# The wait between an up and a down projection: down units begin on ten of eleven hidden tiles

## The chip, the core and the metric

The kernel runs on one core of a Trainium2 chip. Such a core has TensorE (PE in the profile) for matmuls, VectorE (DVE), ScalarE (ACT), GpSimd (POOL) and SyncE (SP), each with its own stream of instructions; they meet at semaphores, and DMA queues bring data from the chip's main memory. The metric is the time of one execution in microseconds on the device; less is better.

## The reference

Two layers of a diffusion backbone over 512 latent tokens and 256 context tokens, of width 1024. Each layer mixes tokens in four parallel branches and then runs a feed-forward network. Only that last part matters here:

```python
def swiglu(u, w_gate_up, w_down):
    gate, up = jnp.split(u @ w_gate_up, 2, axis=-1)
    return (jax.nn.silu(gate) * up) @ w_down

for l in range(DEPTH):                      # DEPTH = 2
    with_ctx = l < DEPTH - 1
    ...
    u = modulate(rmsnorm(h, g_ffn_pre[l]), mod[3], mod[4])
    h = h + mod[5] * rmsnorm(swiglu(u, w_gate_up[l], w_down[l]), g_ffn_post[l])
    if with_ctx:
        ...
        hc = hc + modc[5] * rmsnorm(swiglu(uc, w_gate_up[l], w_down[l]), g_ffn_post[l])
```

The hidden width is 2816, which is 22 tiles of 128. Layer 0 works on all 768 tokens, layer 1 on the 512 latent ones.

## The kernel before

**Numbers in two halves.** Every large product is made of three matmuls: activations and weights are each split into a high part (a copy to the 4-byte type that PE reads fast) and a low part (the value minus the high part), and PE adds high x high, low x high and high x low. This is `chunk_product` (L787 is its matmul), for one block of 128 input rows `k` and one output tile.

**Weight units.** Weights come in units of up to 128 x 2048 values. SP's DMAs bring a unit into one of two raw buffers; ACT makes `w_hi` (L1278) and DVE makes `w_lo` (L1725). Both are in a helper `split(g, it, s)` that each engine has, and that always prepares the unit after the one named: the split of unit u + 1 stands at the head of unit u's work and waits until the products of unit u - 1, which used the same buffer, are done (`acc_ready`) and the transfer has landed. SP brings the unit after that when DVE's `w_lo` has freed the raw buffer.

**The feed-forward stages.** The hidden width is worked in two halves of 11 tiles, so a layer has the phases up0, down0, up1, down1. An up unit (11 in a phase) makes the gate tile (j = 0) and the up tile (j = 1) of one hidden tile. ACT takes SiLU of the gate out of PSUM (L1310), DVE multiplies it with the up tile (L1752), POOL then copies the product to `hid_hi` (L2414), subtracts to get `hid_lo` (L2416) and counts up `hid_split`. A down unit (8 in a phase) makes one output tile of 128 channels from the 11 hidden tiles of its half, in 11 row blocks. Its result is copied out by ACT in down0 (L1342) and added by DVE in down1 (L1779).

**What sets the order.** There is no scheduler: each engine's program is written out, phase by phase. At the end of a phase ACT, DVE and POOL meet at a barrier (`Phases.end`: each counts up `others_end` and waits for all three and for PE). PE only drains and goes on when another product phase follows (`end_products`). Before a down phase PE waits for `hid_split` to reach `g.h0`, the number of all hidden tiles made so far, so for the last tile of the up phase as well (L916). Inside a phase, `pairs` runs units in a hardware loop of two units a turn; with `peel` the first two units are straight code ahead of the loop. PE's products use two accumulators in turn, which ACT or DVE set free (`acc_free`).

**Background.** The up0 phase of layer 0 also computes part of the next layer's modulation: DVE sums, and PE's small matmuls (L770) close each unit and the phase.

Places that the change and the prediction touch: `gemm_unit` and `gemm` of PE, ACT and DVE, `split` of ACT and DVE, and the barrier.

Of the kernel before, what the change touches and what calls it, by code (L numbers as in the profile page):

```python
# [233 lines left out]
def build(nc, x, c, ctx_in, c_ctx, w_mod, b_mod, g_mix_pre, g_mix_post, g_ffn_pre, g_ffn_post, w_in, a_sink,  # L234
# [4 lines left out]
    with stack:  # L239
# [507 lines left out]
        def _(pe):  # L747
# [57 lines left out]
            def gemm_unit(g, it, s, bk, at):  # L805
# [4 lines left out]
                for j in range(g.nt):  # L810
# [3 lines left out]
                    if not early:  # L814
                        if g.t0 >= 2 or t >= 2:
                            pe.wait_ge(acc_free[t % 2], t // 2 + g.nt * it)
                        for k in range(g.kc):
                            if g.name == "uq_nope" and j == 0:
                                made = g.t0 - HEADS + k
                                pe.wait_ge(acc_free[made % 2], made // 2 + 1)  # L820
                            chunk_product(g, slot, t, j, k)
                            order = gate_order(g.layer)
                            if g.name == "gates1_rest" and j == 0 and 0 <= k - (KD - len(order)):
                                gate_block(order[k - (KD - len(order))])
# [86 lines left out]
            def gemm(groups, bk):  # L911
                if groups[0].name == "w_out":
                    early_unit(groups[0])
                for g in groups:
                    if g.name.startswith("down"):
                        pe.wait_ge(hid_split, g.h0)  # L916
                    if g.name == "branch1":
                        pe.wait_ge(y_split, HEADS * (n.ysp + 1))
                        n.ysp += 1
                    pairs(pe, g, lambda it, s: gemm_unit(g, it, s, bk, g.u0 - groups[0].u0), peel=bk is not None)  # L920
                if bk is not None:
                    for i in bk.rest(sum(g.n for g in groups) - 1):
                        back_unit(bk, 0, i)
# [342 lines left out]
        def _(act):  # L1266
# [12 lines left out]

            def gemm_unit(g, it, s):  # L1280
                l = g.layer
                if not (g.early and isinstance(it, int) and 2 * it + s == 0) or g.name == "w_out":
                    split(g, it, s)
                if g.name == "gates1_rest":
                    act.wait_ge(tr_copied, n.tr)
# [92 lines left out]
                if made == 13:  # L1378
                    act.wait_ge(dup_in, 16 * n.dup)

            def gemm(l, groups):
                if groups[-1].name == "branch1":
                    tok = toks(groups[0].lat)
                    for slot in range(2):
# [16 lines left out]
                for g in groups:  # L1401
                    if g.name == "uq_nope":
                        act.wait_ge(c_spread, l + 1)
                        A(tile_at(C_RSTD, False), ps[:, 6:8, 0:TOK // 2], ACT.Copy).then_inc(c_rstd, 1)
                    pairs(act, g, lambda it, s: gemm_unit(g, it, s), peel=g.kind == "swiglu")
                g = groups[-1]
                if g.kind == "merge" and g.dst[0] != 3:

# [236 lines left out]
            n.lstm_w = 0  # L1645
            for index, (kind, l, arg) in enumerate(phases):
                if kind == "gemm":
                    gemm(l, arg)
                elif kind == "setup":
                    load_vectors(act, 0)  # L1650

# [63 lines left out]
        def _(dve):  # L1715
# [3 lines left out]
            def split(g, it, s):  # L1719

                slot, u = (g.u0 + s + 1) % 2, g.u0 + s + 2 * it + 1
                if isinstance(u, int) and u >= n_units:
                    return
                dve.wait_ge(w_hi_done, u + 1)
                V.tensor_tensor(w_lo[slot][:, :], w_raw[slot][:, :], w_hi[slot][:, :].bitcast(F32),  # L1725
                                ALU.subtract).then_inc(w_lo_done, 1)

            def gemm_unit(g, it, s, bk, at):
                if not (g.early and isinstance(it, int) and 2 * it + s == 0) or g.name == "w_out":
                    split(g, it, s)  # L1730
                if bk is not None:
                    static = isinstance(it, int)
# [549 lines left out]
            for index, (kind, l, arg) in enumerate(phases):  # L2282
# [6 lines left out]
                if kind == "gemm":  # L2289
                    bk = background.get(index)  # L2290
                    for g in arg:
# [8 lines left out]
                            if isinstance(it, int) and g.name != "ukv":  # L2300
                                ropes(arg, g.u0 - arg[0].u0 + 2 * it + s)

                        pairs(dve, g, unit, peel=bk is not None)
                    for i in bk.rest(sum(g.n for g in arg)) if bk is not None else ():
                        back_sums(bk, 0, i)
                elif kind == "setup":
# [220 lines left out]
```

## Time and profile before

| | |
|---|---|
| Median of 3 runs | 3462.56 us (3456.1 to 3471.19) |
| Profiled execution, its own time | 3466.68 us |
| Its span, first to last instruction | 3464.9 us |
| PE busy | 3249.9 us, 94% |
| DVE, ACT, POOL busy | 1690.6, 1082.4, 337.9 us |
| Mean granted clock of PE | 0.958 |

The timeline prints runs of equal instructions as one row: start, duration, engine, line, operation, out <- in with the tile's shape, the count, and in brackets how long the engine stood idle just before and who released it. A granted clock of 1 is 2.4 GHz, 0.5 is 1.2 GHz. "768" or "512" in a shape is the number of tokens: layer 0 or layer 1.

### The profile page before, as it was taken

To read this page: it belongs to the slowest core of one execution; us is meant where nothing else is said; L and a number is where in the kernel's file an instruction comes from. 1 tells how busy PE (TensorE), PEld (TensorE's weight loads), DVE (VectorE), ACT (ScalarE), POOL (GpSimd) and SP (SyncE) were. 2 spreads that over 40 slices of the span, in tenths; PEclk is the share of its full clock that TensorE was granted. 3 is DMA by queue.
4 is the path that set the end of the run, shared out by engine and by line. 5 is a ranking of instruction groups with operands and counts; after the bars stand their busy time and mean duration, and the time that the engine had idled before them with its cause. 6 is when DMAs were issued, how large, how long until landed. Compare 5 with 4: busy or idle time off the path is not lost. (4 is left out here: it accounts for less than half of the span.)

```text
span 3464.9 us, 46710 instructions
## 1 busy us (share of the span) xinstructions
PE 3249.9 (94%) x18308; PEld 2934.4 (85%) x18308; DVE 1690.6 (49%) x3070; ACT 1082.4 (31%) x1806; POOL 337.9 (10%) x252
## 2 busy tenths in 40 slices
PE   7999999999999989899999989999999998889997
PEld 4999988998898789899999988877887886677876
DVE  6645355433376765763121365545433577443334
ACT  3233344333314433211211232334443234322222
POOL 0001100100120010121031000010100210101010
PEclk8999999999999998899999989999999999979998
DMA  5511410320250022432221333141321521332322
GB/s 199 174 40 49 131 50 13 122 61 25 74 189 25 25 95 88 146 121 64 76 61 45 95 128 100 61 122 37 110 61 37 183 67 37 134 97 79 110 80 97
DMA packets 332309, 303.79 MB, mean 88 GB/s; under 512 B 39822, under 2 KB 309852, under 8 KB 330204
## 3 DMA queue, kind: packets, MB, share of 16 engines
q1 hardware_dynamic: 317134, 230.03, 21.3%
q10 hardware_dynamic: 14990, 71.23, 5.4%
q8 instruction: 124, 2.03, 0.2%
q14 instruction: 61, 0.50, 0.0%
HBM read 266.47 MB, written 34.34 MB: 87 GB/s over the span
## 5 line engine op out<-in xcount | busy, mean ns | idle before, releaser
L787 PE MATMUL ps<-u_hi,w_hi 128*128 128x384 f32 (+1 forms) x2352 | 687.3, 354 | 40.9 <-issue 19.3
L787 PE MATMUL ps<-u_lo,w_hi 128*128 128x384 f32 (+1 forms) x2352 | 679.2, 350 | 0.0
L787 PE MATMUL ps<-u_hi,w_lo 128*128 128x384 f32 (+1 forms) x2352 | 678.6, 350 | 0.0
L1725 DVE TENSOR_TENSOR w_lo<-w_raw,w_hi 128x2048 fp32r<-128x2048 f32 x145 | 353.2, 2436 | 431.1 <-ACT w_hi L1278 428.9
L787 PEld LDWEIGHTS ps<-u_hi,w_hi 128*128 128x128 f32 x2352 | 430.2, 190 | 70.8 <-issue 45.0
L787 PEld LDWEIGHTS ps<-u_lo,w_hi 128*128 128x128 f32 x2352 | 434.0, 190 | 22.1
L787 PEld LDWEIGHTS ps<-u_hi,w_lo 128*128 128x128 f32 x2352 | 433.3, 190 | 22.8
L1278 ACT ACTIVATE w_hi<-w_raw 128x2048 fp32r<-128x2048 f32 x145 | 277.5, 1914 | 519.6 <-PE ps L787 293.4
L980 PE MATMUL ps<-u_hi,w_hi 128*128 128x384 f32 (+1 forms) x816 | 311.6, 382 | 4.5 <-ACT space L1485 3.5
L980 PE MATMUL ps<-u_hi,w_lo 128*128 128x384 f32 (+1 forms) x816 | 297.1, 364 | 0.0
L980 PE MATMUL ps<-u_lo,w_hi 128*128 128x384 f32 (+1 forms) x816 | 294.9, 361 | 0.0
L1887 DVE SCALAR_TENSOR_TENSOR space<-space,silu_c 128x256 f32<-128x256 f32 x560 | 247.6, 484 | 9.9
L1342 ACT ACTIVATE space<-ps 128x768 f32<-128x768 f32 (+3 forms) x102 | 76.5, 752 | 469.4 <-PE ps L787 457.7
L1057 PEld LDWEIGHTS ps<-space 128*128 128x128 f32 x1472 | 184.4, 196 | 35.0 <-issue 16.5
L1057 PE MATMUL ps<-space 128*128 128x128 f32 (+1 forms) x1472 | 202.1, 284 | 5.4 <-DVE space L2107 4.9
L2065 DVE TENSOR_REDUCE mx<-ps 128x1 f32<-128x768 f32 (+3 forms) x200 | 156.2, 781 | 101.4 <-PE ps L1015 75.7
L1752 DVE TENSOR_TENSOR space<-space,ps 128x768 f32<-128x768 f32 (+1 forms) x44 | 36.1, 821 | 308.7 <-PE ps L787 301.8
L980 PEld LDWEIGHTS ps<-u_hi,w_hi 128*128 128x128 f32 x816 | 156.5, 192 | 19.5 <-issue 7.3
L787 PE MATMUL ps<-hid_hi,w_hi 128*128 128x384 f32 (+1 forms) x528 | 160.7, 358 | 12.1 <-POOL hid_lo L2416 12.1
L980 PEld LDWEIGHTS ps<-u_hi,w_lo 128*128 128x128 f32 x816 | 155.8, 191 | 11.4
L980 PEld LDWEIGHTS ps<-u_lo,w_hi 128*128 128x128 f32 x816 | 156.6, 192 | 7.5
L787 PE MATMUL ps<-hid_lo,w_hi 128*128 128x384 f32 (+1 forms) x528 | 159.7, 356 | 0.0
(264 smaller groups left out, 4537.2 us busy)
## 6 DMA issues: line engine op xcount, KB each, us to landing
w_raw<-in_w_in SPq DMA_DIRECT2D x288, 256.0 KB, 3.9
space<-in_w_mod SPq DMA_DIRECT2D x48, 1024.0 KB, 5.1
w_raw<-in_w_gate_up SPq DMA_DIRECT2D x176, 256.0 KB, 3.8
w_raw<-in_w_down SPq DMA_DIRECT2D x96, 192.0 KB, 2.7
w_raw<-in_w_branch SPq DMA_DIRECT2D x64, 256.0 KB, 3.4
h_scratch<-space ACTq DMA_DIRECT2D x4, 3072.0 KB, 8.6
space<-h_scratch ACTq DMA_DIRECT2D x4, 3072.0 KB, 10.3
m_scratch<-space ACTq DMA_DIRECT2D x3, 3072.0 KB, 9.8
```

Of the source, the lines that this page charges most:

```text
L787: last = nc.tensor.matmul(ps[:, 2 * (t % 2) + b, 0:a1 - a0], wv[w][:, k, j * P:(j + 1) * P], xx[:, k, a0:a1], start=(k == 0 and w == 0 and ...
L980: last = nc.tensor.matmul(ps[:, fill_bank, 0:cols.stop - cols.start], wv[w][:, k, j * P:(j + 1) * P], xx[:, k, cols], start=k == 0 and m = ...
L1057: last = nc.tensor.matmul(ps[:, 6, h * dv:(h + 1) * dv], pt_buf[i % 2][:, bi * P:(bi + 1) * P], v, start=bi == 0, stop=bi == len(keys) - 1)
L1278: A(w_hi[slot][:, :], w_raw[slot][:, :], ACT.Copy).then_inc(w_hi_done, 1)
L1342: A(tile_at(dst_tile(g, it, s, j), g.lat), acc(t % 2, g.lat), ACT.Copy if g.kind == "copy" else ACT.Sigmoid, scale=HD ** -0.5 if g.name == ...
L1725: V.tensor_tensor(w_lo[slot][:, :], w_raw[slot][:, :], w_hi[slot][:, :].bitcast(F32), ALU.subtract).then_inc(w_lo_done, 1)
L1752: V.tensor_tensor(tile_at(30 + s, g.lat), tile_at(30 + s, g.lat), acc(t % 2, g.lat), ALU.mult).then_inc(hid_ready, 1)
L1887: ins = V.scalar_tensor_tensor(part[:, sg], w, silu_c[:, k, sg:sg + 1], part[:, sg], ALU.mult, ALU.add)
L2065: own.did(V.reduce_max(mx[:, c4:c4 + 1], view, AX))
```

## The change

Three engines change at the four passages from an up phase to a down phase.

- PE: the wait ahead of a down phase is for one tile fewer (`g.h0 - 1`). In the first unit of the phase, ahead of the eleventh row block (`k == HALF - 1`, HALF is 11), PE waits for the last tile (`g.h0`).
- ACT and DVE: the split that stood at the head of the first down unit (it prepares the second down unit) is issued at the end of the up phase, ahead of the barrier: `split_next(after)` in ACT, `split(after, 0, 0)` in DVE. The first down unit leaves its own call out.
- PE, ACT and DVE run the first two units of down0 as straight code ahead of the loop (`peel`), so that the first unit can differ. down1 had no loop before either. down1 of layer 1 and of layer 0 are otherwise treated alike.

```diff
@@ -815,6 +815,8 @@
                         if g.t0 >= 2 or t >= 2:
                             pe.wait_ge(acc_free[t % 2], t // 2 + g.nt * it)
                         for k in range(g.kc):
+                            if g.name.startswith("down") and k == HALF - 1 and isinstance(it, int) and it == s == 0:
+                                pe.wait_ge(hid_split, g.h0)
                             if g.name == "uq_nope" and j == 0:
                                 made = g.t0 - HEADS + k
                                 pe.wait_ge(acc_free[made % 2], made // 2 + 1)
@@ -913,11 +915,12 @@
                     early_unit(groups[0])
                 for g in groups:
                     if g.name.startswith("down"):
-                        pe.wait_ge(hid_split, g.h0)
+                        pe.wait_ge(hid_split, g.h0 - 1)
                     if g.name == "branch1":
                         pe.wait_ge(y_split, HEADS * (n.ysp + 1))
                         n.ysp += 1
-                    pairs(pe, g, lambda it, s: gemm_unit(g, it, s, bk, g.u0 - groups[0].u0), peel=bk is not None)
+                    pairs(pe, g, lambda it, s: gemm_unit(g, it, s, bk, g.u0 - groups[0].u0),
+                          peel=bk is not None or g.name.startswith("down"))
                 if bk is not None:
                     for i in bk.rest(sum(g.n for g in groups) - 1):
                         back_unit(bk, 0, i)
@@ -1279,7 +1282,8 @@
 
             def gemm_unit(g, it, s):
                 l = g.layer
-                if not (g.early and isinstance(it, int) and 2 * it + s == 0) or g.name == "w_out":
+                first = isinstance(it, int) and 2 * it + s == 0
+                if not first or not (g.early or g.name.startswith("down")) or g.name == "w_out":
                     split(g, it, s)
                 if g.name == "gates1_rest":
                     act.wait_ge(tr_copied, n.tr)
@@ -1378,7 +1382,10 @@
                 if made == 13:
                     act.wait_ge(dup_in, 16 * n.dup)
 
-            def gemm(l, groups):
+            def split_next(g):
+                split(g, 0, 0)
+
+            def gemm(l, groups, after):
                 if groups[-1].name == "branch1":
                     tok = toks(groups[0].lat)
                     for slot in range(2):
@@ -1402,7 +1409,10 @@
                     if g.name == "uq_nope":
                         act.wait_ge(c_spread, l + 1)
                         A(tile_at(C_RSTD, False), ps[:, 6:8, 0:TOK // 2], ACT.Copy).then_inc(c_rstd, 1)
-                    pairs(act, g, lambda it, s: gemm_unit(g, it, s), peel=g.kind == "swiglu")
+                    pairs(act, g, lambda it, s: gemm_unit(g, it, s),
+                          peel=g.kind == "swiglu" or g.name.startswith("down"))
+                    if g.kind == "swiglu":
+                        split_next(after)
                 g = groups[-1]
                 if g.kind == "merge" and g.dst[0] != 3:
 
@@ -1645,7 +1655,7 @@
             n.lstm_w = 0
             for index, (kind, l, arg) in enumerate(phases):
                 if kind == "gemm":
-                    gemm(l, arg)
+                    gemm(l, arg, groups_of(phases[index + 1])[0] if groups_of(phases[index + 1]) else None)
                 elif kind == "setup":
                     load_vectors(act, 0)
 
@@ -1726,7 +1736,8 @@
                                 ALU.subtract).then_inc(w_lo_done, 1)
 
             def gemm_unit(g, it, s, bk, at):
-                if not (g.early and isinstance(it, int) and 2 * it + s == 0) or g.name == "w_out":
+                first = isinstance(it, int) and 2 * it + s == 0
+                if not first or not (g.early or g.name.startswith("down")) or g.name == "w_out":
                     split(g, it, s)
                 if bk is not None:
                     static = isinstance(it, int)
@@ -2300,7 +2311,10 @@
                             if isinstance(it, int) and g.name != "ukv":
                                 ropes(arg, g.u0 - arg[0].u0 + 2 * it + s)
 
-                        pairs(dve, g, unit, peel=bk is not None)
+                        pairs(dve, g, unit, peel=bk is not None or g.name.startswith("down"))
+                        if g.kind == "swiglu":
+                            after = groups_of(phases[index + 1])[0]
+                            split(after, 0, 0)
                     for i in bk.rest(sum(g.n for g in arg)) if bk is not None else ():
                         back_sums(bk, 0, i)
                 elif kind == "setup":
```

PE at the first passage, up0 to down0 of layer 0, before (L770 closes up0; `hid_hi` and `hid_lo` are the halves of the hidden tiles; L177 is `pairs`' loop):

```order
L787 MATMUL ps<-u_lo,w_hi 128x384 x2
L787 MATMUL ps<-u_hi,w_lo 128x384 x2
L770 MATMUL ps<-ones,space 128x1 [waits back_summed]
L770 MATMUL ps<-ones,space 128x1 x3
L770 MATMUL ps<-ones,space 128x1 [waits back_summed]
L770 MATMUL ps<-ones,space 128x1 x3
L177 UNCONDITIONAL_BRANCH [waits hid_split]
L177 ISA
L816 REGISTER_ALU [waits w_lo_done]
L787 MATMUL ps<-hid_hi,w_hi 128x384 [waits acc_free1]
L787 MATMUL ps<-hid_hi,w_hi 128x384
```

and of the change:

```order
L787 MATMUL ps<-u_lo,w_hi 128x384 x2
L787 MATMUL ps<-u_hi,w_lo 128x384 x2
L770 MATMUL ps<-ones,space 128x1 [waits back_summed]
L770 MATMUL ps<-ones,space 128x1 x3
L770 MATMUL ps<-ones,space 128x1 [waits back_summed]
L770 MATMUL ps<-ones,space 128x1 x3
L787 MATMUL ps<-hid_hi,w_hi 128x384 [waits acc_free1,w_lo_done,hid_split]
L787 MATMUL ps<-hid_hi,w_hi 128x384
L787 MATMUL ps<-hid_lo,w_hi 128x384 x2
L787 MATMUL ps<-hid_hi,w_lo 128x384 x2
```

The loop's entry is gone from here, and the three waits stand on the first down matmul; which value of `hid_split` is meant is in the diff. Further down in the same unit of the change, at the eleventh row block:

```order
L787 MATMUL ps<-hid_hi,w_hi 128x384 x2
L787 MATMUL ps<-hid_lo,w_hi 128x384 x2
L787 MATMUL ps<-hid_hi,w_lo 128x384 x2
L787 MATMUL ps<-hid_hi,w_hi 128x384 [waits hid_split]
L787 MATMUL ps<-hid_hi,w_hi 128x384
L787 MATMUL ps<-hid_lo,w_hi 128x384 x2
L787 MATMUL ps<-hid_hi,w_lo 128x384 x2
L787 MATMUL ps<-hid_hi,w_hi 128x384 [waits acc_free0,w_lo_done]
```

Here the second wait for `hid_split` has come in, ahead of the last six matmuls of the unit; the row that waits for `w_lo_done` begins the second down unit.

ACT at the second passage, up1 to down1 of layer 0, before:

```order
L177 COMPARE_AND_BRANCH
L1278 ACTIVATE w_hi<-w_raw 128x2048 [waits acc_ready,w_landed0]
L1310 ACTIVATE space<-ps 128x768 [waits hid_split,acc_ready]
L1278 ACTIVATE w_hi<-w_raw 128x2048 [waits gate_silu,w_landed1,acc_ready,pe_end,others_end]
L1428 ACTIVATE space<-space 128x768 [waits sums_ready,acc_free1]
L1355 ACTIVATE space<-space,gain 128x256 [waits square_done]
L1355 ACTIVATE space<-space,gain 128x512
L1278 ACTIVATE w_hi<-w_raw 128x2048 [waits acc_ready,w_landed0]
```

and of the change:

```order
L177 COMPARE_AND_BRANCH
L1281 ACTIVATE w_hi<-w_raw 128x2048 [waits acc_ready,w_landed0]
L1314 ACTIVATE space<-ps 128x768 [waits hid_split,acc_ready]
L1281 ACTIVATE w_hi<-w_raw 128x2048 [waits gate_silu,acc_ready,w_landed1]
L1438 ACTIVATE space<-space 128x768 [waits acc_free1,sums_ready,pe_end,others_end]
L1359 ACTIVATE space<-space,gain 128x256 [waits square_done]
L1359 ACTIVATE space<-space,gain 128x512
L1281 ACTIVATE w_hi<-w_raw 128x2048 [waits acc_ready,w_landed0]
```

The weight copy that follows the last SiLU has lost its waits for `pe_end` and `others_end`, the barrier; they stand on the squares of the first down tile now. DVE's `w_lo` moves with it in the same way.

## Rows read from the trace of the kernel before

**Rows 1.** the page's first part: busy us, share of the span, instructions

```profile
PE 3249.9 (94%) x18308; PEld 2934.4 (85%) x18308; DVE 1690.6 (49%) x3070; ACT 1082.4 (31%) x1806; POOL 337.9 (10%) x252
```

**Rows 2.** waits of PE: line, releaser: us in total, times, longest us

```profile
PE ps L787 <- POOL hid_lo L2416: 12.1, 4, 3.8
```

**Rows 3.** timeline, first place (up0 to down0, layer 0): start us, us, engine, line, operation [idle]

```profile
1590.68 0.81 ACT L1310 ACTIVATE space<-ps 128x768 f32<-128x768 f32 x1 [7.23 <-PE ps L787]
...
1598.81 1.84 PE L770 MATMUL ps<-ones,space 128*128 128x1 f32 x16
1599.01 0.95 DVE L1752 TENSOR_TENSOR space<-space,ps 128x768 f32<-128x768 f32 x1 [4.70 <-PE ps L787]
1600.93 1.80 POOL L2416 TENSOR_TENSOR hid_lo<-space,hid_hi 128x768 fp32r<-128x768 f32 x1
...
1603.06 1.91 ACT L1278 ACTIVATE w_hi<-w_raw 128x2048 fp32r<-128x2048 f32 x1 [11.56 <-POOLq L418]
1603.06 1.00 PE L787 MATMUL ps<-hid_hi,w_hi 128*128 128x384 f32 x2 [2.41 <-POOL hid_lo L2416]
```

**Rows 4.** timeline, second place (up1 to down1, layer 0)

```profile
1879.41 0.51 PE L787 MATMUL ps<-u_hi,w_lo 128*128 128x384 f32 x2
...
1881.88 1.80 POOL L2416 TENSOR_TENSOR hid_lo<-space,hid_hi 128x768 fp32r<-128x768 f32 x1
...
1883.73 1.01 PE L787 MATMUL ps<-hid_hi,w_hi 128*128 128x384 f32 x2 [3.81 <-POOL hid_lo L2416]
```

**Rows 5.** timeline, third place (up0 to down0, layer 1)

```profile
3187.45 0.49 PE L787 MATMUL ps<-hid_hi,w_hi 128*128 128x512 f32 x1 [3.07 <-POOL hid_lo L2416]
```

**Rows 6.** timeline, fourth place (up1 to down1, layer 1)

```profile
3370.80 0.80 PE L787 MATMUL ps<-hid_hi,w_hi 128*128 128x512 f32 x1 [2.80 <-POOL hid_lo L2416]
```

**Rows 7.** timeline, down0 to up1 in layer 0 and in layer 1

```profile
1696.59 0.60 PE L787 MATMUL ps<-u_hi,w_hi 128*128 128x384 f32 x2 [0.44 <-issue]
...
3248.04 0.49 PE L787 MATMUL ps<-u_hi,w_hi 128*128 128x512 f32 x1 [0.44 <-issue]
```

**Rows 8.** stretches of up0 (layer 0) and behind the four places

```profile
core 0: us, PE busy (x) PEld busy (x) DVE busy (x) ACT busy (x) POOL busy (x), PEclk, DMA share, GB/s
1453.00:1600.00 147.00, 147.00 (x877) 147.00 (x876) 96.88 (x154) 21.85 (x16) 36.57 (x16) 1.00 0.34 108
1603.00:1606.00 3.00, 2.94 (x9) 2.95 (x10) 1.38 (x4) 1.91 (x1) 0.00 (x0) 0.52 0.00 0
1883.70:1889.20 5.50, 5.47 (x17) 5.47 (x18) 2.29 (x1) 1.91 (x1) 0.00 (x0) 0.50 0.02 4
3187.40:3190.40 3.00, 2.95 (x13) 2.44 (x14) 0.99 (x1) 1.92 (x1) 0.00 (x0) 1.00 0.00 0
3370.80:3374.00 3.20, 3.20 (x8) 2.52 (x9) 1.10 (x1) 1.91 (x1) 0.00 (x0) 0.50 0.00 0
```

**Rows 9.** timeline of ACT: tile copies of down0, layer 0, then layer 1

```profile
1627.65 0.81 ACT L1342 ACTIVATE space<-ps 128x768 f32 x1 [8.83 <-PE ps L787]
...
1639.08 0.81 ACT L1342 ACTIVATE space<-ps 128x768 f32 x1 [8.81 <-PE ps L787]
...
3202.88 0.60 ACT L1342 ACTIVATE space<-ps 128x512 f32 x1 [5.10 <-PE ps L787]
...
3210.34 0.60 ACT L1342 ACTIVATE space<-ps 128x512 f32 x1 [5.05 <-PE ps L787]
```

**Rows 10.** timeline, inside up1 of layer 0, then inside up0 of layer 1

```profile
1763.56 0.95 DVE L1752 TENSOR_TENSOR space<-space,ps 128x768 f32<-128x768 f32 x1 [12.49 <-PE ps L787]
...
1765.42 2.29 DVE L1725 TENSOR_TENSOR w_lo<-w_raw,w_hi 128x2048 fp32r<-128x2048 f32 x1 [0.91 <-ACT w_hi L1278]
1765.68 3.75 POOL L2416 TENSOR_TENSOR hid_lo<-space,hid_hi 128x768 f32 x1 [0.16 <-POOL hid_hi L2414]
...
3142.86 3.23 DVE L1725 TENSOR_TENSOR w_lo<-w_raw,w_hi 128x2048 fp32r<-128x2048 f32 x1 [1.17 <-ACT w_hi L1278]
```

**Rows 11.** timeline, PE behind the norm ahead of up0, layer 0

```profile
1400.02 0.98 PE L787 MATMUL ps<-u_hi,w_hi 128*128 128x384 f32 x2 [5.42 <-issue]
```

## The prediction

> **What bounds the kernel now.** The page's first part comes first: TensorE (PE) is busy 94% of the span and no other engine reaches half [rows 1]. So only time in which PE stands still, or runs at the lower clock, can be won. The list of waits by engine and line then says what PE waits for. For the change one line counts: the matmuls of L787 (the products of every weight unit) waited for POOL's instruction at L2416, the second half of the split of a feed-forward tile, 12.1 us in total, in 4 waits, the longest 3.8 us [rows 2]. A third view, the timeline, shows where: at the four places at which an up projection's stage ends and a down projection's begins, two a layer [rows 3 to 6]. The chain is the same each time: last matmul of the up stage, DVE's product of the two halves of the gate (L1752), POOL's copy (L2414) and POOL's difference (L2416), then the first down matmul. PE stands 2.41, 3.81, 3.07 and 2.80 us. At the first of the four, 1.84 us of background products (L770) run first, which is why its gap is the shortest although the chain is as long as at the second.
>
> **The wait that goes.** The new threshold lets PE begin with ten of the eleven row blocks of the unit; the last tile's split is wanted only at the eleventh. What is left of each gap is what PE pays between two such stages when it waits for nothing. The trace has this too, at the two places where down0 ends and up1 begins: 0.44 us each [rows 7]. So the gain is 12.1 - 4 x 0.44 = 10.3 us. If a straight entry into the stage costs nothing it is 12.1; if the background products in front of the first place make the step dearer, it can be a few tenths less than 10.3. I take 10.3.
>
> **The cover for the split.** A down unit over all 768 tokens takes 11.43 us between its tile copies (66 matmuls, 0.173 us each), one over 512 tokens 7.46 us (33 matmuls, 0.226 us each) [rows 9]. Ten elevenths are 10.4 and 6.8 us; with the 0.44 us of the step, PE reaches the new wait 10.8 or 7.2 us after the last up matmul. The split is complete after about 3.8 and 3.1 us now, as the gaps say. The change makes it later in one way: the weight split of the second down unit, DVE's 2.29 us (L1725), used to start after the phase's barrier, when POOL was done; now it follows DVE's gate product at once, beside POOL's difference. Inside the up stage this meeting already happens each unit: POOL's difference takes 3.75 us there instead of 1.80, and is done 1765.68 + 3.75 - 1763.56 = 5.9 us after DVE's product began [rows 4, 10]. That is under 10.8. Over 512 tokens the nearest row shows DVE as the loser (3.23 instead of 2.29 us) and, if POOL lost, 3.1 + 2.3 = 5.4 is under 7.2. So the new wait costs 0, with 1.8 us of slack at the tighter pair of places. One rule speaks against the edit. The Trainium skill, SBUF — State Buffer, section SBUF: two separate sides, says that a VectorE operation with two inputs in SBUF and a GpSimd one that reads SBUF lock a shared port pair against each other, and that the later one stands still until the first is done. The trace agrees with it in both directions (3.75 against 1.80 us, 3.23 against 2.29), and even the full block leaves the sum as it is, since it falls inside the cover.
>
> **The moved weight split.** ScalarE's copy (1.91 us) and DVE's difference (2.29 us) are no new work: the same two instructions leave the head of the down stage and stand at the end of the up stage. Before, ScalarE stood at the barrier behind POOL and began at 1603.06 [rows 3]; now it begins when the last up tile is complete, some 4 us earlier. The unit it prepares is needed 11.4 or 7.5 us after the first begins, so before the change this was hidden too: gain 0, and without it PE would also not have waited. It does let the weight transfer of the down unit two further on start 4 us earlier; nobody waits for that one, so 0. Barrier: the three other engines now reach it after DVE's 2.29 us, at worst some 2 us after POOL's end of before; PE does not wait there, and ScalarE's next work is the copy of the first down tile 7 us or more away. Cost 0. Peeling the first two units of down0 out of the loops adds straight code on PE, ScalarE and DVE; up0 has run peeled all along and shows no gap at its passage from straight code to loop. Cost 0, at most the gap priced among the rivals.
>
> **The clock.** The second term is not in any wait. After three of the four gaps PE's granted clock is at its lower level (1.2 GHz): 0.52 in the first 3.0 us, 0.50 for 5.5 us, 1.00 at the third, 0.50 for 3.2 us [rows 8]. In these stretches 9, 17 and 8 matmuls begin. At the higher level (2.4 GHz) there would be 2.94/0.173 = 17, 5.47/0.173 = 31.6 and 3.20/0.226 = 14.2. What was lost is 8.0 x 0.173 = 1.4, 14.6 x 0.173 = 2.5 and 6.2 x 0.226 = 1.4 us, together 5.3 us. After the 0.44 us gaps the matmuls come at the full rate at once (durations 0.60 for two and 0.49 for one, against 1.00 and 0.80 after the long ones) [rows 3, 6, 7]. The background products stand in every unit of up0 too, and 1453 to 1600 is at 1.00 throughout [rows 8], so they alone don't lower it. I count all 5.3 us as won. The bounds are 0 (the lower clock comes at some other place instead; of four similar gaps one had no drop, so chance has a part) and 10 (four times the worst, 2.5: another run of the kernel before may have been hit so at each gap). By the Trainium skill, TensorE: Matmul & The Clock Gate, section "Wait — 56ns, not 53.3ns?", matmuls of 384 columns start every 320 ns at the low and 162.5 ns at the high level; with that full rate in place of the row's 173 ns the clock term would be an estimated 5.8 us, half a microsecond more. The trace has 0.32 us too in the slow stretch and is slower than the page in the fast one; the rows decide.
>
> **The sum.** 10.3 + 5.3 = 15.6 us. The profiled execution took 3466.68 us (its span 3464.9), so it would take 3451.1. It lies 4.1 us above the median of the runs shown, 3462.56, and all the stretches concerned are bound by PE, so I take the same 15.6 off the median: 3447.0 us, 0.45% less. The shown runs lie 15 us apart (3456.1 to 3471.19), as much as the whole gain.
>
> **Rivals.** (A) Only the wait goes and the clock does not come back, or comes back here and is lost elsewhere. For it: the third gap shows that a gap needn't cost clock, so the 5.3 us are partly luck. Against it: three of four, and none at the short gaps. Then 3462.56 - 10.3 = 3452.3. (B) The wait only moves: POOL's split comes too late for the eleventh block, or PE still stands at the head for another semaphore. For it: the collision above. Against it: 5.9 against 10.8 us, and the accumulator bank that the head also waits for is set free by ScalarE's SiLU, done at 1591.5, 7.5 us before the last up matmul ends, and the first unit's weights are split a unit ahead [rows 3]. To win nothing the split would have to end 15 or 10 us after the up stage. Time 3462.6. (C) The other side: PE runs from the end of the up stage into straight code that isn't there yet. Before, any such delay would have lain inside the wait for POOL. The nearest row of a PE gap that the profile gives to nothing but issue is 5.42 us at 1400.02 [rows 11]. At four places that is 21.7 us in place of 12.1, so with the lost clock unchanged 3462.56 + 9.6 = 3472 us. It decides against the change from 3.0 us a place. Against it: that row stands at a norm where data is being made, and down1 was straight code before, too, and began 0.05 us after POOL's difference ended (1883.73 against 1881.88 + 1.80) [rows 4].
>
> **How the numbers follow.** Chances: forecast 0.70, A 0.19, B 0.06, C 0.05. About 0.5%, 17.3 us, is what a measurement of this kernel can tell from no change, and the forecast is 1.7 us short of it: scatter of a median of a few runs, some 4 to 5 us, and a clock term that may be larger put some 0.31 of the forecast's 0.70 beyond it, with 0.02 of A. So faster 0.33; slower is C, nearly whole, 0.05; within 0.62. The range goes from 3438, which is the full 12.1 us and a clock term of 10 with 2 us of scatter (or one of 5.3 with 7), to 3458, which is case A with 6 us of scatter.
>
> **What would show it.** In the profile after, the list of waits has no line of L787 waiting for POOL's difference, and the first down matmul starts about 0.4 us after the last up matmul (the last background product at the first place). The granted clock is 1.00 in the first 5 us of all four down stages. ScalarE's weight copy starts with DVE's gate product, and POOL's last difference takes up to 3.8 us. PE's busy time falls by about 5 us (matmuls at the low clock last longer) and its idle time by 10. The prediction is wrong if PE stands over 1 us at a head or at the eleventh block, or if the low clock shows up within the next few microseconds all the same.

## The result, and the profile after

| | before | changed |
|---|---|---|
| Median | 3464.98 us (8 runs, 3456.1 to 3471.19) | 3446.63 us (8 runs, 3438.94 to 3454.32) |
| Ratio | | 0.9945, 95% interval [0.9934, 0.9956] |
| Span of the profiled execution | 3464.9 us | 3437.2 us |
| PE busy | 3249.9 us | 3233.0 us |

The change takes 19 us off (15 to 23 by the interval); the forecast was 15.6. The page's first part after the change, as in [rows 1]:

```profile
PE 3233.0 (94%) x18308; PEld 2922.5 (85%) x18308; DVE 1694.8 (49%) x3070; ACT 1081.4 (31%) x1806; POOL 340.5 (10%) x252
```

In the list of PE's waits the line of [rows 2] is gone. What grew is the line without a releaser, from 20.3 us in 19 waits to

```profile
PE ps L787 <- issue: 21.4, 23, 5.4
```

Four waits more and 1.1 us: the four heads. The timeline at the first place shows one of them (start, duration, engine, line; compare [rows 3]):

```profile
1591.18 1.84 PE L770 MATMUL ps<-ones,space 128*128 128x1 f32 x16
1591.38 0.95 DVE L1763 TENSOR_TENSOR space<-space,ps 128x768 f32<-128x768 f32 x1 [4.69 <-PE ps L787]
1591.44 1.91 ACT L1281 ACTIVATE w_hi<-w_raw 128x2048 fp32r<-128x2048 f32 x1 [7.56 <-PE ps L787]
...
1593.29 0.59 PE L787 MATMUL ps<-hid_hi,w_hi 128*128 128x384 f32 x2 [0.26 <-issue]
1593.30 1.84 POOL L2430 TENSOR_TENSOR hid_lo<-space,hid_hi 128x768 fp32r<-128x768 f32 x1
1593.38 3.91 DVE L1735 TENSOR_TENSOR w_lo<-w_raw,w_hi 128x2048 fp32r<-128x2048 f32 x1 [1.05 <-ACT w_hi L1281]
```

PE starts the down unit 0.26 us after the background products, while POOL is only beginning its difference. ScalarE's weight copy runs beside DVE's product. POOL's difference got in 0.08 us ahead of DVE's, kept its 1.84 us, and it is DVE's that was stretched, to 3.91 us. The other three places, as in [rows 4 to 6]:

```profile
1869.14 0.59 PE L787 MATMUL ps<-hid_hi,w_hi 128*128 128x384 f32 x2 [0.26 <-issue]
...
3163.84 0.47 PE L787 MATMUL ps<-hid_hi,w_hi 128*128 128x512 f32 x1 [0.26 <-issue]
...
3344.63 0.47 PE L787 MATMUL ps<-hid_hi,w_hi 128*128 128x512 f32 x1 [0.27 <-issue]
```

The stretches behind them, as in [rows 8] (granted clock in the third column from the end): 17, 32, 13 and 14 matmuls begin where 9, 17, 13 and 8 began before, and the clock is 1.00 each time.

```profile
1593.30:1596.30 3.00, 3.00 (x17) 3.00 (x18) 2.92 (x1) 0.05 (x1) 1.84 (x1) 1.00 0.00 0
1869.10:1874.60 5.50, 5.46 (x32) 5.49 (x33) 4.44 (x2) 1.79 (x1) 2.68 (x2) 1.00 0.01 3
3163.80:3166.80 3.00, 2.96 (x13) 2.48 (x14) 1.68 (x2) 1.79 (x1) 1.90 (x2) 1.00 0.00 0
3344.60:3347.80 3.20, 3.17 (x14) 2.65 (x15) 1.88 (x2) 1.78 (x1) 1.90 (x2) 1.00 0.00 0
```

**Where the 27.7 us between the two spans went.** The feed-forward stages of a layer run from PE's first product of up0 to its first instruction behind down1. The rows that bound them, before (what is not in the rows above), layer 0's end and layer 1's start and end:

```profile
1981.15 0.42 PE L930 MATMUL ps<-zeros,ident 128*128 128x6 f32 x2 [3.10 <-ACTq L418]
...
3057.76 0.77 PE L787 MATMUL ps<-u_hi,w_hi 128*128 128x512 f32 x1 [4.97 <-issue]
...
3434.63 0.39 PE L930 MATMUL ps<-zeros,ident 128*128 128x6 f32 x2 [2.21 <-ACTq L418]
```

and after:

```profile
1391.79 0.98 PE L787 MATMUL ps<-u_hi,w_hi 128*128 128x384 f32 x2 [5.42 <-issue]
...
1964.00 0.59 PE L933 MATMUL ps<-zeros,ident 128*128 128x6 f32 x2 [3.10 <-ACTq L418]
...
3037.02 0.76 PE L787 MATMUL ps<-u_hi,w_hi 128*128 128x512 f32 x1 [4.97 <-issue]
...
3406.97 0.39 PE L933 MATMUL ps<-zeros,ident 128*128 128x6 f32 x2 [2.22 <-ACTq L418]
```

Layer 0: 581.13 to 572.21 us, layer 1: 376.87 to 369.95. Together 958.00 to 942.16, 15.8 us less. In these stages PE's busy time fell from 934.05 to 929.12 us and its idle time from 23.95 to 13.04. The other 11.9 us lie where the two programs do the same. Up to the first product of up0 PE has the same work, and yet gets there at 1400.02 before and 1391.79 after; the granted clock of that stretch is 0.96 in one and 0.97 in the other:

```profile
0.00:1400.02 1400.02, 1306.13 (x7957) 1208.44 (x7958) 729.14 (x1537) 475.52 (x925) 110.96 (x95) 0.96 0.26 86
```

```profile
0.00:1391.79 1391.79, 1297.63 (x7958) 1204.17 (x7958) 728.80 (x1537) 474.82 (x925) 113.43 (x95) 0.97 0.26 87
```

So two profiles differ by 8.2 us over the same instructions, in step with the granted clock, and a comparison of whole spans would have credited the change with 27.7.

**The down stages by themselves.** The gaps lie ahead of the first down matmul, so the length of a down stage, from that matmul to the first matmul of what follows, holds no gap that the change removed, and where no wait lies inside it, as in these two kernels, it shows what the clock costs. The starts before are in [rows 3 to 7] and above; after the change the two up1 stages start at

```profile
1685.54 0.61 PE L787 MATMUL ps<-u_hi,w_hi 128*128 128x384 f32 x2 [0.47 <-issue]
...
3224.40 0.49 PE L787 MATMUL ps<-u_hi,w_hi 128*128 128x512 f32 x1 [0.44 <-issue]
```

| us | down0, layer 0 | down1, layer 0 | down0, layer 1 | down1, layer 1 | sum |
|---|---|---|---|---|---|
| before | 93.53 | 97.42 | 60.59 | 63.83 | 315.37 |
| changed | 92.25 | 94.86 | 60.56 | 62.34 | 310.01 |
| less | 1.28 | 2.56 | 0.03 | 1.49 | 5.36 |
| forecast | 1.4 | 2.5 | 0 | 1.4 | 5.3 |

The gaps (11.0 us) and the down stages (5.4) come to 16.4. The 0.6 us to the measured 15.8 were lost inside up0 of layer 0, which took 201.24 us up to the gap at its end in place of 200.63.

### The profile page after: what moved, and what is told of

Same layout as the page of the kernel before. It is cut to its first block and busy times, and to the rows that moved or that the text cites. A ratio compares the mean times of both kernels' runs of the same rounds, so it can differ in the third digit from the quotient of the medians.

```text
span 3437.2 us, 46681 instructions
## 1 busy us (share of the span) xinstructions
PE 3233.0 (94%) x18308; PEld 2922.5 (85%) x18308; DVE 1694.8 (49%) x3070; ACT 1081.4 (31%) x1806; POOL 340.5 (10%) x252
```

## The experiments

Each kernel was timed in five rounds against the kernel before on the same chip; "less" and "more" are ratios times 3464. The stage sums are taken from one profile of each kernel as above: all feed-forward stages (before 958.0, changed 942.2) and the four down stages alone (before 315.4, changed 310.0).

| kernel | median us | ratio [95%] | all stages | down stages | PE's new or old wait |
|---|---|---|---|---|---|
| PE part alone | 3444.03 | 0.9951 [0.9938, 0.9964] | 941.4 | 310.0 | none |
| split part alone | 3467.85 | 1.0007 [0.9996, 1.0018] | 958.5 | 315.9 | 12.1, 4 times |
| wait at the third block | 3448.24 | 0.9964 [0.9950, 0.9977] | 945.4 | 313.9 | 3.1, 3 times |
| gap filled with work | 3455.92 | 0.9978 [0.9967, 0.9988] | 949.9 | 310.1 | 0.8, 2 times |
| split 5 copies late | 3447.94 | 0.9947 [0.9930, 0.9964] | 945.1 | 314.0 | 1.8, 2 times |
| split 12 copies late | 3478.96 | 1.0038 [1.0025, 1.0050] | 971.6 | 340.1 | 19.3, 4 times |
| PE part, 5 copies late | 3457.70 | 0.9973 [0.9960, 0.9986] | 951.8 | 320.4 | 7.1 for w_lo |
| tables early | 3442.17 | 0.9927 [0.9911, 0.9943] | 940.5 | 310.0 | none |
| the change again | 3450.81 | 0.9953 [0.9936, 0.9970] | 941.5 | 310.0 | none |
| tables early again | 3440.11 | 0.9933 [0.9918, 0.9947] | 940.9 | 310.0 | none |

### The two halves of the change

```diff
 PE part alone: before.py with
-                        pe.wait_ge(hid_split, g.h0)
+                        pe.wait_ge(hid_split, g.h0 - 1)
+                            if g.name.startswith("down") and k == HALF - 1 and isinstance(it, int) and it == s == 0:
+                                pe.wait_ge(hid_split, g.h0)
 and PE's peel (lines left out); ACT and DVE untouched
```

> The kernel before with the PE part of the change alone (wait for one hidden tile fewer, the rest at the eleventh block, first two units of down0 straight); ScalarE's and DVE's split of the second down unit stays at the head of the down phase, behind the barrier. Theory (the moved split wins nothing): PE's four gaps are 0.26 us each and the ratio to before is that of the change, 0.9945 within 0.1%. The split is then done 8.2 us (768 tokens) and 7.3 us (512 tokens) after the last up matmul and wanted after 11.7 and 7.7. Rival (the moved split is needed): PE waits for DVE's w_lo ahead of the second down unit, over 1 us at the two places of layer 1, and the gain is 3 us or more smaller (ratio 0.9955 or above).

It has the whole gain: 17 us less (12 to 21), gaps of 0.26 us, stages of 941.4 us. DVE's `w_lo` for the second down unit ends at 3176.81 at the first place of layer 1:

```profile
3174.52 2.29 DVE L1728 TENSOR_TENSOR w_lo<-w_raw,w_hi 128x2048 fp32r<-128x2048 f32 x1 [4.33 <-ACT w_hi L1281]
```

PE began the phase at 3169.74 and wants it 7.46 us later, at 3177.2: 0.4 us to spare.

The other half is the change with PE's waits and loops put back.

> The change without its PE part: the split of the second down unit is made at the end of the up phase, but PE waits for all hidden tiles at the head, as before. Theory: nothing is won, PE's four waits for POOL's difference sum to 12 to 16 us (more than 12.1 only if DVE's w_lo gets ahead of POOL's difference and holds it up), ratio 0.999 to 1.002. Rival (the moved split is part of the gain): ratio under 0.998.

As the theory said: ratio 1.0007, and

```profile
PE ps L787 <- POOL hid_lo L2428: 12.1, 4, 3.8
```

is the old line. POOL was not held up, since it was again in first.

### Is it the wait or the clock?

```diff
 gap filled with work: before.py with, ahead of the old wait,
+                        pe.wait_ge(w_lo_done, g.u0 + 1)
+                        for _ in range(10 if g.lat else 11 if g.name == "down0" else 18):
+                            nc.tensor.matmul(ps[:, 6, 0:SEQ if g.lat else TOK // 2], w_hi[g.u0 % 2][:, 0:P],
+                                             u_hi[:, 0, CTX_LEN:TOK] if g.lat else u_hi[:, 0, 0:TOK // 2],
+                                             start=True, stop=True)
                         pe.wait_ge(hid_split, g.h0)
```

> The kernel before, with its waits as they were, but PE makes 11, 18, 10 and 10 extra matmuls (results unused, written to a bank that nobody reads) at the four heads ahead of the wait for POOL: 1.9, 3.1, 2.3 and 2.3 us of work inside gaps of 2.41, 3.81, 3.07 and 2.80 us. This leaves the time at which PE goes on and takes away the idleness alone. Theory (the second term of the gain is the clock behind the gaps): granted clock 1.00 at all four places, 4 to 8 us less than before, ratio 0.9985 +- 0.001. Rival (the whole gain is the wait, the low clock would come in any case): ratio 1.000 and stretches at 0.5 behind the gaps.

This kernel does 49 matmuls more than before, starts its down stages no earlier, and takes 7.6 us less (4 to 11). At the second place:

```profile
1882.00 3.39 PE L918 MATMUL ps<-u_hi,w_hi 128*128 128x384 f32 x18
1885.74 0.44 PE L787 MATMUL ps<-hid_hi,w_hi 128*128 128x384 f32 x1 [0.35 <-POOL hid_lo L2421]
```

and behind it and the others the clock stays up:

```profile
1604.00:1610.00 6.00, 5.86 (x32) 5.54 (x33) 2.29 (x4) 1.92 (x1) 1.90 (x2) 1.00 0.00 0
1885.70:1891.20 5.50, 5.46 (x31) 5.46 (x32) 2.29 (x1) 1.92 (x1) 0.00 (x0) 1.00 0.00 0
3180.30:3183.30 3.00, 3.00 (x13) 2.49 (x14) 1.06 (x1) 1.91 (x1) 0.00 (x0) 1.00 0.00 0
3363.60:3366.80 3.20, 3.16 (x14) 2.62 (x15) 1.06 (x1) 1.92 (x1) 0.00 (x0) 1.00 0.00 0
```

The low clock behind the gaps was the gaps' doing, and its price is a term of its own. Its size is best read from the down stages of this profile: 92.25, 94.90, 60.58 and 62.36 us, together 5.3 us less than before, place by place what the change itself has. The median's 7.6 us can't be split that finely. In this profile another 2.8 us lie inside up0 of layer 1, where the granted clock of the first 6.6 us is 0.77 and not 0.58 as before; nothing in the edit touches that place.

The next kernel lets PE begin as in the change, but has it wait for the last tile much sooner.

> The change with the wait for the last hidden tile ahead of the third row block in place of the eleventh, so that PE works 2.1 us (768 tokens) or 1.4 us (512 tokens) and then stands. POOL is ready 3.8 us after the last up matmul in layer 0 (2.4 after the background products at the first place) and about 3.0 in layer 1, so the gaps should be 4 x 0.26 at the heads and about 0.1, 1.4, 1.4 and 1.1 inside: 5.1 us in all, 7 us less than before. Theory (lower clock follows long gaps only): the clock term comes back nearly whole, so 7 + 4 to 8 us less than before, ratio 0.9965 +- 0.0012, and the granted clock is 1.00 behind at least three of the four places. Rival (the clock reacts to how much PE idles in a stretch, however cut up): half the term stays lost, ratio 0.9975 or above, and the clock is at 0.5 behind two or more places.

The edit: the change's `k == HALF - 1` is `k == 2` here. It takes 12.5 us less than before (8 to 17), as the theory had it. The waits at the third block are 1.24, 0.91 and 0.92 us, none at the first place, 3.1 where 4.0 were counted, and no low clock at any of the four. Each wait still costs 0.3 us more than its length: the three down stages took 1.52, 1.21 and 1.19 us longer than in the change.

### How thick is the cover?

```diff
 the change, with in POOL's body (range(12 ...) in the second kernel)
                             pool.wait_ge(hid_ready, hid + 1)
+                            for _ in range(5 if k == HALF - 1 else 0) if isinstance(k, int) else ():
+                                own.did(G.tensor_copy(hid_lo[:, kk, tok], src))
+                                own.wait()
```

> The change, with five extra copies by POOL ahead of the split of the last hidden tile of each up phase (some 4.4 us over 768 tokens, 3.4 over 512; what they write is overwritten by the split). The split is then complete about 8.2 and 6.4 us after the last up matmul. Theory (ten blocks cover 10.7 and 7.1 us): PE's gaps stay at 0.26 us, and the time is that of the change within 0.1%, ratio to before 0.9945. Rival (the cover is thinner than counted, or the later barrier costs PE): a wait of L787 for POOL or DVE of over 1 us at one or more places, ratio 0.996 or above.

In layer 0 no wait appears. In layer 1 the expectation of no wait failed by a little: 0.92 and 0.91 us at the eleventh block, since the five copies took 5.38 us and not 3.4. DVE's weight split ran in the middle of them at its full speed (2.29 us), and POOL stood about as long (it takes 0.62 us for such a copy alone):

```profile
3172.18 5.38 POOL L2429 CAST hid_lo<-space 128x512 fp32r<-128x512 f32 x5 [8.60 <-DVE space L1763]
3173.44 2.29 DVE L1735 TENSOR_TENSOR w_lo<-w_raw,w_hi 128x2048 fp32r<-128x2048 f32 x1 [1.32 <-ACT w_hi L1281]
...
3179.65 0.50 PE L787 MATMUL ps<-hid_hi,w_hi 128*128 128x512 f32 x1 [0.92 <-POOL hid_lo L2433]
```

PE reached the wait at 3179.65 - 0.92 = 3178.73, 7.1 us after its start at 3171.65. Ten blocks had been counted as 6.8, so the cover is what was counted, and 0.3 us more. The time, 0.9947, can't be told from the change's, though the down stages are 4.0 us longer in the profile. Of these 2.4 are the two waits and what follows them. The other 1.5 lie at the first place, where something came that the change does not show: PE's gap at the head is 0.26 us as in the change, and all the same the clock fell behind it.

```profile
1599.10:1602.10 3.00, 2.94 (x11) 2.95 (x12) 2.84 (x1) 0.13 (x1) 2.87 (x3) 0.61 0.00 0
```

> As the kernel before it in this list, but twelve extra copies (some 10.6 and 8.2 us): the split is complete about 14.4 and 11.2 us after the last up matmul. Theory: PE stands at the eleventh block for 3.7 us at the second place, some 2 at the first (the background products come on top of the cover there), and 4.1 us at the two of layer 1, 14 us in all, so the gain is gone: 12 to 18 us more than the change, ratio 0.998 to 1.001. The low clock returns behind at least one place. Rival (the barrier, reached that late, costs more than the wait): further waits of PE for the second or third down unit, ratio over 1.002.

32 us more than the change where 12 to 18 were expected. The waits are 19.3 us, not 14 (the twelve copies took 12.60 and 10.15 us), and behind all four the clock is down:

```profile
1616.40:1619.40 3.00, 2.94 (x11) 2.94 (x12) 0.56 (x3) 0.99 (x2) 0.01 (x1) 0.60 0.00 0
1899.60:1905.10 5.50, 5.42 (x20) 5.42 (x21) 0.95 (x1) 1.83 (x3) 0.03 (x1) 0.62 0.00 0
3201.70:3204.70 3.00, 3.00 (x7) 2.44 (x8) 0.00 (x0) 1.23 (x2) 0.00 (x0) 0.50 0.00 0
3391.20:3394.40 3.20, 3.13 (x7) 2.51 (x8) 0.69 (x1) 0.49 (x1) 0.01 (x1) 0.50 0.03 5
```

The stages grew by 29.5 us: 19.3 of waits, and about 10 that are mostly low clock. Here too the clock was already down once behind the head of the first place, ahead of the wait, with a gap of 0.26 us:

```profile
1603.40:1607.00 3.60, 3.60 (x13) 3.60 (x12) 1.49 (x1) 0.00 (x0) 3.47 (x3) 0.53 0.15 45
```

There is no later wait in the down stages, so the late barrier by itself cost PE nothing. The ratio is over the 1.002 of the rival, but the further waits that the rival needs are not there.

> The PE part alone (ScalarE's and DVE's split of the second down unit stays behind the barrier) with the same five extra copies as in the first kernel of this list. Theory (the moved split buys independence of the barrier, which the PE part alone has 0.4 us of in layer 1): the weight split is done about 12.5 us after the last up matmul in layer 0 and 10.8 in layer 1, wanted at 11.7 and 7.7; PE waits for DVE's w_lo about 0.8 us at the second place and 3.1 at each of the two of layer 1, 7 us together, ratio 0.996 to 0.998. Rival (the moved split does nothing even then): the same time as the first kernel of this list.

As the theory said: 0.9973, and the wait is for DVE's weight split, in the one of the three late kernels that has it behind the barrier:

```profile
PE ps L787 <- DVE w_lo L1728: 7.1, 4, 2.8
```

(one of the four, 0.9 us, is an older one elsewhere; the others are 0.84, 2.79 and 2.62). Behind the two long ones the clock was down again, at the first of them

```profile
3186.20:3191.20 5.00, 5.00 (x15) 3.94 (x16) 2.18 (x1) 0.00 (x0) 0.00 (x0) 0.66 0.69 198
```

Against the first kernel of this group, equal but for the moved split, it is 9 us slower (0.9947 to 0.9973; the intervals overlap by a hair, but both stand against the same runs of before, and the difference of 0.26% clears the 0.21% that the two intervals make together; the stage sums differ by 6.6 us). So the second half of the change is an insurance: no gain shows while POOL is on time, and several microseconds do when it is late.

### The activation tables loaded early

On ScalarE the trace has rows `ACT_TABLE_LOAD`, 1.28 us each, where it passes from one function to another such as SiLU or Exp. In the change's profile one of them stands directly ahead of the first SiLU of up0, behind the wait for PE:

```profile
1411.37 1.28 ACT L1314 ACT_TABLE_LOAD   x1 [5.43 <-PEq L424]
```

This version lets a one-element activation pull the load forward to where ScalarE has nothing to do (lines between the places are left out):

```diff
+        warm = sb("warm", [P, 1])
 ACT, ahead of the end of norm_ffn:
+                    if kind == "norm_ffn":
+                        A(warm[:, :], zeros[:, 0:1], ACT.Silu)
 ACT, at the start of attend() and of mlstm():
+                A(warm[:, :], zeros[:, 0:1], ACT.Exp)
```

> The change plus nine tiny activations of one element a partition (six Exp at the start of the attention phases, one at the start of each mLSTM phase, one SiLU ahead of the end of each feed-forward norm; eleven table loads are meant to move by them: in the profile of the change ScalarE loads a table for 1.28 us directly ahead of the first SiLU of up0, where PE stands 2.41 and 2.20 us, and ahead of the first Exp of an attention, where PE stands up to 4.6 us). Theory: the loads go beside other waits, up to 1.28 us less at each of the two SiLU places and at some of the others, 3 to 10 us less than the change, ratio to before 0.992 to 0.994. Rival (they were hidden, or only swap places with the next wait): ratio as the change, 0.9945.

(The ten activations are six, two and two.) PE's gap ahead of the second unit of up0 in layer 0 went from

```profile
1413.66 0.59 PE L787 MATMUL ps<-u_hi,w_hi 128*128 128x384 f32 x2 [2.41 <-ACTq L1317]
```

in the change to

```profile
1418.83 0.58 PE L788 MATMUL ps<-u_hi,w_hi 128*128 128x384 f32 x2 [1.13 <-ACTq L1318]
```

with four more like it, but the next gap in the same stage grew from 1.16 to 4.30 us. So both were run again side by side:

> The change itself once more, beside the next kernel, so that both stand against the same runs of before. Its gain is 11.0 us of gaps (12.1 less four times 0.26) and a clock term that the busy-gap kernel gave as 7.6 us (3.9 to 11.4 by its interval): ratio 0.9945 +- 0.0008. If the first measurement was lucky, 0.9955, which is what my forecast of 15.6 us says.

> The change with the ten tiny activations that load ScalarE's tables early, once more. Theory: the five places at which its profile shows shorter PE gaps (2.41 to 1.13, 2.20 to 0.92, 2.94 to 1.59, 3.21 to 1.91, 4.60 to 3.41 us) are worth 6.4 us less what comes back elsewhere: 2 to 7 us less than the change, ratio to before 0.9925 to 0.994. Rival: the same time as the change, since DVE's waits for the modulation weights and the first feed-forward tile end when they did (one gap in its profile grew from 1.16 to 4.30 us).

0.9953 and 0.9933. The change again is nearer to the 0.9955 of my forecast than to its own first 0.9945; its interval holds both. In the tables version the grown gap is there again, 4.07 us where the change beside it has 1.02:

```profile
1414.14 0.61 DVE L1902 TENSOR_SCALAR space<-space,silu_c 128x256 f32<-128x256 f32 x2 [9.04 <-DMA space<-in_w_mod]
...
1422.46 1.01 PE L788 MATMUL ps<-u_hi,w_hi 128*128 128x384 f32 x2 [4.07 <-DVEq L1772]
```

DVE stands until a modulation weight has come, does its sums, and only then takes the tile that frees PE's accumulator. That weight came 24.4 us after up0 began here and 24.2 us in the change, so PE, earlier by the saved load, only meets this wait earlier, and behind the long gap its granted clock is 0.50 for 5.8 us, where the change has 1.00. So up0 of layer 0 got 2.9 us longer and up0 of layer 1, which has no such wait, 3.5 us shorter. All feed-forward stages together are under 1 us shorter than in the change beside it; what else is won must lie outside them, and no run separates it.

Both pairs put the tables 0.18 to 0.20% ahead of the change, some 6 to 7 us. Each pair alone doesn't clear its intervals; the two together do narrowly (0.19% +- 0.15%). Against the kernel before it is 23 to 25 us faster.

## Why the prediction was right

**The wait that goes: right, a little more than counted.** 10.3 us were forecast from steps of 0.44 us; they are 0.26, 0.26, 0.26 and 0.27, so 12.1 - 1.05 = 11.0. The 0.44 us rows [rows 7] are entries into a loop, the new heads are straight code; that difference was named as a bound and not chosen.

**The clock: right, in kind and in size.** 5.3 us were counted from matmuls that began too late. The down stages of the pair of profiles give 5.4, place by place what was counted (1.28, 2.56, 0.03 and 1.49 against 1.4, 2.5, 0 and 1.4), and the kernel with filled gaps gives 5.3 with the waits still there. The two views that the prediction named, PE's busy time down by about 5 us and its idle time by 10, hold in the feed-forward stages (4.9 and 10.9); the page's busy time fell by 16.9, the rest of it where the programs do the same. Rival A, that the low clock would only come elsewhere, had 0.19. In the two profiles of the change and in that of the PE part alone it did not come, and filling the gaps alone pays. It was not an idle thought, though: with the split five and twelve copies late the low clock did come behind a head of 0.26 us, and cost 1.5 us in the first of them. The side estimate of 5.8 us for this term, on which nothing rests, comes to 5.6 when it is worked as the 5.3 was.

**The cover: right.** 10.7 and 7.1 us with the shorter step; the late splits show the wait appear within 0.3 us of where the sum puts it. What I had wrong is who loses where POOL and DVE meet. I took POOL, as in up1 of layer 0 [rows 10], and allowed 3.8 us for its difference. At all four heads POOL was first, by under 0.6 us, and DVE paid (3.91 and 2.9 instead of 2.29 us). So the last tile's split was done 3.8 us after DVE's product began in layer 0 and 2.7 in layer 1, and not 5.9 and 5.4. It was of no account to the sum, as the prediction had it for either order.

**The moved split: right that it wins nothing, too short on why.** I wrote that it was hidden before too. It was, but in layer 1 the PE part alone has 0.4 us of slack, and PE starting earlier is what made it so thin. The prediction did not work that figure out, and it is the reason to have that half of the change.

**The other rivals.** B, the wait only moves: no wait at the eleventh block in the change. C, straight code not there when PE needs it: the heads are 0.26 us and shorter than a loop entry, so no. No kernel has the straight code of down0 without the earlier start, so what it does by itself is read only from the length of the steps.

**The total, with some luck.** The time was put at 3447.0 and measured as 3446.63, but the two agree better than the working does. The medians lie 18.4 us apart and not 15.6; the kernel before, in eight runs, was at 3464.98 and not at the 3462.56 from which the 15.6 were taken, and these 2.4 us hide most of the difference. The stages of the profiles give 15.8, the repeat of the change 16 by its ratio.

**The chances.** A gain over 0.5% was given 0.33. It came out at 0.55% the first time and 0.47% the second: truly on the line, as said.

## What to carry to other kernels

A gap on a bound engine is worth more than its length when the engine's clock falls behind it: read the granted clock of the few microseconds after the gap, and count the instructions that start there. A wait on a whole group of inputs can often be split so that only the last one holds up the last step of the first product; what it then needs is a cover longer than the producer's chain, and the chain must be taken with its collisions. Measure such a change by the stages that it touches: two profiles can differ by 8 us where the programs are the same. When one wait goes, work out the slack of the next one in line, here the second unit's weights, even where it does not bind yet.

## What the runs showed of the hardware

A gap's length alone does not say whether the low clock comes behind it, nor for how long. With the same gaps at the same four places (2.41, 3.81, 3.07, 2.80 us), before had 0.52, 0.50, 1.00 and 0.50 behind them [rows 8], and the kernel with the split part alone

```profile
1607.90:1610.90 3.00, 2.97 (x9) 2.97 (x10) 2.41 (x4) 0.00 (x0) 0.00 (x0) 0.50 0.00 0
1890.10:1895.60 5.50, 5.47 (x22) 5.47 (x23) 2.13 (x1) 0.00 (x0) 0.00 (x0) 0.69 0.36 100
3192.20:3195.20 3.00, 2.92 (x13) 2.45 (x14) 1.91 (x1) 0.00 (x0) 0.00 (x0) 1.00 0.00 0
3375.60:3378.80 3.20, 3.20 (x8) 2.52 (x9) 2.09 (x1) 0.00 (x0) 0.00 (x0) 0.50 0.00 1
```

that is, less of it at the second place (22 matmuls begin in the 5.5 us instead of 17, and the stage takes 96.5 us instead of 97.4) and more at the first (the stage takes 95.1 us instead of 93.5). In sum it lost 5.9 us and before 5.4. The gap of 3.07 us had no low clock behind it in either, while the wait of 2.79 us in the PE part with five copies had. The four waits of 2.34 to 5.69 us of the twelve copies had it behind each, the five waits of 0.91 to 1.24 us behind none.

A short gap is not safe either. At the first place PE does 1.84 us of one-column background products, stands 0.26 us and goes on. Behind this the clock stayed at 1.00 in seven profiles of nine (the change twice, the PE part alone and with five copies, the third block, the tables twice); in the two with the late split and the moved weight split it fell to its lower level, for 3.6 us. Which difference between them brings that, or whether it is chance, no run shows.

Where DVE's difference of two tensors in SBUF (the on-chip memory) and a POOL instruction that reads SBUF overlap, the one that started later stands while the other runs, in both directions: POOL's took 3.75 us inside up1 [rows 10]. A lead of less than 0.1 us decides: POOL's difference began at 1593.30, DVE's at 1593.38 and ended 2.15 us after POOL's end, where alone it takes 2.29. The Trainium skill, SBUF — State Buffer, section SBUF: two separate sides, says so, and that whoever starts first decides; the trace agrees.
